# Sparse attention of a whole-model kernel: the order of its first heads, and the turn of the weights by diagonals of gate over sum

## The reference, cut to what matters

```python
s_c = q . kc * scale + bias_c;  p_c = softmax(where(valid_c, s_c, NEG_INF)) * any_c;  o_c = p_c @ vc
s   = q . ks * scale + bias;    o_s = softmax(s) @ vs        # selected blocks: all of the past
s   = q . kw * scale + bias_w;  o_w = softmax(s) @ vw        # window of 512: all of the past
gt  = sigmoid(gates)
o   = gt[..., 0:1] * o_c + gt[..., 1:2] * o_s + gt[..., 2:3] * o_w
```

## Time and profile before

| what | us |
|---|---|
| median of 3 runs | 3545.63 (3542.86 to 3548.09) |
| profiled execution | 3545.68 |
| its span, first to last instruction | 3543.9 |
| TensorE busy | 3438.5 (97%) |
| VectorE busy | 2297.3 (65%) |
| ScalarE busy | 1788.3 (50%) |

### The profile page before, as it was taken

The page is one execution under the profiler, slowest core; times in us unless marked ns, Lnnn a source line. Parts: engine busy times, 40 slices in busy tenths (PEclk is TensorE's granted clock), DMA queues, the critical chain, the costliest instruction groups (busy, mean ns, idle before and its releaser), DMA issues.

```text
span 3543.9 us, 62898 instructions
## 1 busy us (share of the span) xinstructions
PE 3438.5 (97%) x21968; PEld 2998.0 (85%) x21968; DVE 2297.3 (65%) x3449; ACT 1788.3 (50%) x2742; POOL 489.5 (14%) x538
## 2 busy tenths in 40 slices
PE   9998999999999999999999999999489999999999
PEld 7886888888888888887888888888378888888888
DVE  5788565555555766775666677778855765565565
ACT  4477464545454554553555444444444554444454
POOL 0001410111114100123100001105012000001105
PEclk9999999999999999999999999999899999999999
DMA  6562545565556555553456556667235455555555
GB/s 212 172 184 61 190 151 192 186 191 185 190 183 194 170 188 170 162 168 119 145 193 197 187 189 196 202 222 246 59 125 186 147 190 191 185 187 193 181 187 195
DMA packets 190644, 626.52 MB, mean 177 GB/s; under 512 B 26822, under 2 KB 40328, under 8 KB 190360
## 3 DMA queue, kind: packets, MB, share of 16 engines
q1 hardware_dynamic: 179948, 612.29, 53.9%
q10 hardware_dynamic: 10572, 12.56, 1.2%
HBM read 620.32 MB, written 3.15 MB: 176 GB/s over the span
## 4 chain that ended last, share of the span: by engine, by line
PE 88%; DVE 7%; ACT 2%; DMA 1%; issue 1%; POOL 0%; SPq 0%; ACTq 0%; DVEq 0%; POOLq 0%
PE bank L1943 54%; PE bank L1946 28%; PE m L1966 1%; DVE w_lo L1073 1%; DMA w_raw<-stream 1%; PE m L1956 1%; PE m L1968 1%; DVE prod L1749 1%; ACT w_hi L481 0%; DVE st L1752 0%; DVE st L1754 0%; DVE y L1100 0%; DVE w_lo L1077 0%; ACT s_first L666 0%; ACT u_own L972 0%
## 5 line engine op out<-in xcount | busy, mean ns | idle before, releaser
L1073 DVE TENSOR_TENSOR w_lo<-w_raw,w_hi 128x1024 fp32r<-128x1024 f32 x1086 | 1336.4, 1253 | 776.5 <-ACT w_hi L481 770.2
L1943 PE MATMUL bank<-act,w_hi 128*128 128x512 f32 x6016 | 1512.8, 393 | 3.6 <-DVE w_lo L1073 1.6
L481 ACT ACTIVATE w_hi<-w_raw 128x1024 fp32r<-128x1024 f32 x1090 | 1129.5, 1054 | 409.8 <-PE bank L1946 362.6
L1943 PEld LDWEIGHTS bank<-act,w_hi 128*128 128x128 f32 x6016 | 1082.7, 189 | 204.6 <-DVE w_lo L1073 4.3
L1946 PEld LDWEIGHTS bank<-act,w_lo 128*128 128x128 f32 x6016 | 820.8, 190 | 58.9
L1946 PE MATMUL bank<-act,w_lo 128*128 128x256 f32 x6016 | 838.7, 282 | 0.0
L1943 PE MATMUL bank<-ffn,w_hi 128*128 128x512 f32 x2432 | 613.5, 393 | 4.0 <-DVE w_lo L1077 2.7
L490 ACT ACTIVATE low<-bank 128x256 f32<-128x256 f32 x542 | 207.5, 383 | 745.0 <-PE bank L1946 744.1
L1943 PEld LDWEIGHTS bank<-ffn,w_hi 128*128 128x128 f32 x2432 | 436.2, 189 | 83.2 <-DVE w_lo L1077 5.0
L1946 PEld LDWEIGHTS bank<-ffn,w_lo 128*128 128x128 f32 x2432 | 333.9, 190 | 25.1
L1081 DVE TENSOR_TENSOR ev<-bank,low 128x256 f32<-128x256 f32 x468 | 198.2, 423 | 236.7 <-ACT low L490 233.3
(11 more groups left out here) (425 smaller groups left out, 2236.8 us busy)
## 6 DMA issues: line engine op xcount, KB each, us to landing
w_raw<-stream SPq DMA_DIRECT2D x1148, 512.0 KB, 3.5
b_part<-s_bt ACTq DMA_DIRECT2D x16, 256.0 KB
bias<-toeplitz SPq DMA_DIRECT2D x4, 512.0 KB, 9.1
pow_b<-powers ACTq DMA_DIRECT2D x8, 256.0 KB
pow_b<-powers ACTq DMA_DIRECT2D x16, 128.0 KB
res<-x_t SPq DMA_DIRECT2D x2, 512.0 KB, 9.0
res<-x_t ACTq DMA_DIRECT2D x2, 512.0 KB, 11.0
bias<-toeplitz SPq DMA_DIRECT2D x4, 256.0 KB, 11.7
```

The costliest lines, as they stand in the source:

```text
L481: a(w_hi[:, q, :], w_raw[:, q, :], ACT.Copy).then_inc(hi_ready, 1)
L1073: e.tensor_tensor(w_lo[:, q, :], w_raw[:, q, :], w_hi[:, q, :].bitcast(F32), ALU.subtract).then_inc(lo_ready, 1)
L1943: mm(bank[w][:, 0:2 * n], w_hi[:, q, wt], x(h * hk + k, 0, 2 * n), start=(h == 0 and k == 0), stop=False)
```

## The change

- Bias: SP loads the bias in two steps. The part of the first four heads (`FIRST_HEADS`) goes out between the first and the second load of the last `cmp` pair, the rest behind that pair. VectorE waits for each part only where it is used.
- Order ahead of the loop: pair 0's scores come ahead of the compression's matmuls on TensorE, and pair 1's behind them. The compression's results go into bank `m[4]`, the gates into `m[5]`. The sum of the LRU's squares is made during and right behind the compression, and the root is taken ahead of the gelu. VectorE splits a weight quarter ahead of the LRU's product.
- Order in the loop: VectorE is one head further: iteration `it` makes the scores and maxima of head `it + 1`, and head 0's come ahead of the loop. TensorE issues a pair's scores ahead of a turn instead of behind it. Copying the compressed keys and values comes behind head 0's exponentials, the compressed scores around head 0's turn, and their softmax in iterations 2 and 3. Compressed weights are turned ahead of heads 2, 3, 5, 7, 9, 11, 13 and 15 (`TURN_AFTER`).
- The turn: the weights keep their exponentials. VectorE makes four 128x128 diagonals a head (`scaler`, identity times factor, one 128x512 instruction, two heads' worth of memory), and TensorE multiplies each block of the exponentials with its diagonal, as an ordinary fp32 matmul.
- The fillers behind the compressed scores (22) and ahead of head 1's turn (10) are gone.

```diff
--- before
+++ after
...
+    scaler = at("scaler", A + 70, [P, 2, 4, P])
...
     score_bank = [m[0:2], bank]
+    FIRST_HEADS = 4
+    TURN_AFTER = (2,) + tuple(range(3, NH, 2))
...
-            sp_eng.wait_ge(halves_used, 4 * PH["in1"][1])
-            sp_eng.wait_ge(sem("toep_out"), 16)
-            for lo_c, hi_c, off in ((128, 384, 127), (0, 128, 255)):
-                for p0 in range(0, P, ROWS):
-                    src = bass.AP(toeplitz.tensor, off - p0, [[383, ROWS], [384 * ROWS, NH], [1, hi_c - lo_c]])
-                    sp_eng.dma_start(bias[p0:p0 + ROWS, :, lo_c:hi_c], src).then_inc(sem("bias_loaded"), 16)
+
+            def load_bias(h0, h1, into):
+                for lo_c, hi_c, off in ((128, 384, 127), (0, 128, 255)):
+                    for p0 in range(0, P, ROWS):
+                        src = bass.AP(toeplitz.tensor, off - p0 + 384 * ROWS * h0,
+                                      [[383, ROWS], [384 * ROWS, h1 - h0], [1, hi_c - lo_c]])
+                        sp_eng.dma_start(bias[p0:p0 + ROWS, h0:h1, lo_c:hi_c], src).then_inc(into, 16)
+
+            for q in range(4):
+                sp_eng.wait_ge(lo_ready, 4 * (after_in1 - 1) + (q - 3))
+                load(after_in1 - 1, q)
+                if q == 0:
+                    sp_eng.wait_ge(halves_used, 4 * PH["in1"][1])
+                    sp_eng.wait_ge(sem("toep_out"), 16)
+                    load_bias(0, FIRST_HEADS, sem("bias_steps"))
+            load_bias(FIRST_HEADS, NH, sem("bias_loaded"))
...
+            hi(c0 + 1, 0)
             block_high(1)
...
-            hi(c0 + 1, 0)
+            hi(c0 + 1, 1)
+            hi(c0 + 1, 2)
             lru_square(0, 3)
-            hi(c0 + 1, 1)
-            lru_square(3, 6)
-            hi(c0 + 1, 2)
-            lru_square(6, 8)
             hi(c0 + 1, 3)
+            lru_square(3, 8)
+            root_table()
+            norm("lru", z, 8, lru_n, LT * P, None)
             hidden(0)
             hidden(1)
             a(counted[:, 0:1], eps_col[:, :], ACT.Copy).then_inc(low_copied, 4)
+            a(exp_use[:, :], eps_col[:, :], ACT.Exp)
...
-            root_table()
-            s.wait_ge(sem("blk_ready"), 1)
-            s.wait_ge(sem("cmp_mm"), 3)
...
-            a(v_cmp[:, :], m[4][0:NCMP, 64:320], ACT.Copy).then_inc(sem("cmp_cp"), 1)
-            norm("lru", z, 8, lru_n, LT * P, None)
-            a(exp_use[:, :], eps_col[:, :], ACT.Exp)
+
+            def compressed_copies():
...
+                s.wait_ge(sem("cmp_mm"), 3)
...
+                a(v_cmp[:, :], m[4][0:NCMP, 64:320], ACT.Copy).then_inc(sem("cmp_cp"), 1)
...
+                if hh in TURN_AFTER:
+                    j = TURN_AFTER.index(hh)
+                    s.wait_ge(sem("pct_mm"), j + 1)
...
                 if it == 0:
+                    compressed_copies()
+                if it == 3:
                     s.wait_ge(sem("cmp_vec"), 3)
                     a(p_cmp[:, :, :], p_cmp[:, :, :], ACT.Exp).then_inc(sem("cmp_exp"), 1)
...
+            lo(c0, 3)
...
             e.tensor_tensor(z[:, 0:LT, :], lru_i[:, :, :], z[:, LT:2 * LT, :], ALU.mult).then_inc(sem("lru_vec"), 1)
-            c0 = PH["cmp"][0]
-            lo(c0, 3)
+            lo(c0 + 1, 0)
             block_low(1)
-            lo(c0 + 1, 0)
...
+            def score(hh):
+                if hh == 0:
+                    v.wait_ge(sem("bias_steps"), 16 + 32 * P // ROWS)
+                if hh == FIRST_HEADS:
+                    v.wait_ge(sem("bias_loaded"), 32 * P // ROWS)
+                if hh >= 4:
+                    v.wait_ge(sem("pt_mm"), 2 * hh - 6)
+                for at_ in range(2):
+                    v.wait_ge(sem("s_mm"), 4 * (hh // 2) + 2 * at_ + hh % 2 + 1)
+                    e.scalar_tensor_tensor(s_att(hh)[:, at_, :], score_bank[hh % 2][at_][:, 0:384], HD ** -0.5, bias[:, hh, :],
+                                           ALU.mult, ALU.add).then_inc(sem("s_bias"), 1)
+
...
+            v.wait_ge(sem("tok_cp"), 3)
+            score(0)
+            top(0)
+            top_negated(0)
             for it in range(NH + 1):
 
-                b, o = it % 2, (it + 1) % 2
-                if it < NH:
-                    if it >= 4:
-                        v.wait_ge(sem("pt_mm"), 2 * it - 6)
-                    for at_ in range(2):
-                        v.wait_ge(sem("s_mm"), 4 * (it // 2) + 2 * at_ + b + 1)
-                        e.scalar_tensor_tensor(s_att(it)[:, at_, :], score_bank[b][at_][:, 0:384], HD ** -0.5, bias[:, it, :], ALU.mult, ALU.add).then_inc(sem("s_bias"), 1)
+                o = (it + 1) % 2
+                if it + 1 < NH:
+                    score(it + 1)
                 if it:
                     v.wait_ge(sem("att_exp"), it)
                     e.reciprocal(stat[:, 112 + 8 * o:116 + 8 * o], stat[:, 96 + 8 * o:100 + 8 * o]).then_inc(sem("att_inv"), 1)
-                if it < NH:
-                    v.wait_ge(sem("s_bias"), 2 * it + 2)
...
+                if it + 1 < NH:
+                    top(it + 1)
...
-                if it < NH:
-                    v.wait_ge(sem("att_top"), 2 * it + 2)
...
-                if it == 0:
-                    compressed()
+                if it + 1 < NH:
+                    top_negated(it + 1)
+                if it == 3:
+                    compressed_weights()
                 if it == 3:
                     lo(c0 + 2, 0)
                 if it:
                     v.wait_ge(sem("att_fac"), it)
-                    for qb, c in enumerate((slice(0, 128), slice(128, 384))):
-                        f = stat[:, 128 + 8 * o + 2 * qb:130 + 8 * o + 2 * qb]
-                        e.tensor_tensor(s_att(it - 1)[:, :, c], s_att(it - 1)[:, :, c],
-                                        f.unsqueeze(2).to_broadcast([P, 2, c.stop - c.start]), ALU.mult).then_inc(sem("att_p"), 1)
-
+                    if it >= 3:
+                        v.wait_ge(sem("pt_mm"), 2 * it - 4)
+                    e.tensor_tensor(scaler[:, o, :, :], ident[:, :].unsqueeze(1).to_broadcast([P, 4, P]),
+                                    stat[:, 128 + 8 * o:132 + 8 * o].unsqueeze(2).to_broadcast([P, 4, P]), ALU.mult).then_inc(sem("att_p"), 1)
+                if it == 2:
+                    compressed_scores()
                 if it == 3:
                     v.wait_ge(root_taken, n_lru)
...
+            pe.wait_ge(sem("lru_sig"), 2 * LT)
+            pair_scores(0)
...
+            for kv in range(2):
+                pe.wait_ge(sem("blk_ready"), kv + 2)
+                i = PH["cmp"][0] + kv
+                into = m[4][0:60, T * kv:T * kv + T]
+                for q in range(4):
+                    if kv and q == 3:
+                        pe.wait_ge(sem("tok_cp"), 3)
+                        lru_sum(0, 3)
+                    pe.wait_ge(lo_ready, 4 * i + q + 1)
...
+                    for n in range(4):
...
+                        mm(into, high, w_hi[:, q, wt], start=(k == 0), stop=False)
...
+            lru_sum(3, 8)
+            pair_scores(1)
...
-            lru_sum(0, 2)
             turn_hidden(1)
-            pair_scores(0)
             pe.wait_ge(sem("cmp_cp"), 2)
-            pe.wait_ge(sem("tok_cp"), 3)
...
-            lru_sum(2, 8)
-            pe.wait_ge(sem("cmp_cp"), 5)
-            for b in range(2):
...
-            last.then_inc(sem("cmp_scores"), 1)
-            keep_busy(22)
+                if b:
+                    last.then_inc(sem("cmp_scores"), 1)
...
-                if hh == 1:
-                    keep_busy(10, m[4])
                 if hh == NH - 1:
                     keep_busy(8, m[0])
-                pe.wait_ge(sem("att_p"), 2 * hh + 2)
...
                     for n in range(3):
-                        last = nc.tensor.transpose(m[2 + at_][:, 128 * n:128 * n + 128], s_att(hh)[:, at_, 128 * n:128 * n + 128], ident[:, :])
+                        last = mm(m[2 + at_][:, 128 * n:128 * n + 128], s_att(hh)[:, at_, 128 * n:128 * n + 128],
+                                  scaler[:, hh % 2, 2 * (n > 0) + at_, :], start=True, stop=True)
                     last.then_inc(sem("pt_mm"), 1)
...
             for it in range(NH + 2):
+                if it == 1:
+                    compressed_scores(0)
+                if it and it % 2 == 0 and it + 2 < NH:
+                    pair_scores(it // 2 + 1)
                 if 1 <= it <= NH:
-                    if it % 2:
-                        cmp_weights(it // 2)
+                    if it - 1 in TURN_AFTER:
+                        cmp_weights(TURN_AFTER.index(it - 1))
                     transposes(it - 1)
-                if it % 2 == 0 and it + 2 < NH:
-                    pair_scores(it // 2 + 1)
+                if it == 1:
+                    compressed_scores(1)
...
```

More of the change, by code:

```diff
@@ L421, in _ @@
         if "mix1" in plan:
-            with sp_eng.Fori(2, after_in1) as i:
+            with sp_eng.Fori(2, after_in1 - 1) as i:
                 for q in range(4):
@@ L1295, in _ @@
             block_low(0)
```

(54 more changed lines are left out.)

40 lines of the change are left out of this document (24 added, 16 removed).

## The result

| | us |
|---|---|
| before, median of 8 runs | 3545.04 (3540.97 to 3548.09) |
| after, median of 8 runs | 3553.87 (3551.79 to 3558.98) |
| ratio | 1.0026, 95% interval 1.0017 to 1.0035 |
| profiled execution of after, its span | 3553.73, 3551.9 |

The change costs 8.8 us (8.05 between the two profiled executions). The forecast was +4.0, the rival *the clock stays down* +9.9. The time is in the range, but nearer to that rival. At 0.26% above before it falls among the outcomes slower by over 0.2%, which the prediction had given 0.23.

The account below looks back on a forecast made before the run. The bias transfer bounds the start, and VectorE and ScalarE, waiting for each other, the loop. The terms 0.7 + 1.15 + 2.0 + 0.2 = 4.0 on 3545.68 gave 3549.7 us, range 3540 to 3558.

Parts of the forecast that it names:

- the clock stays down: Rival: 1.2 GHz from the compressed scores to pair 1's result costs 6 and 3.4 us; 3555.6 us; chance 0.20.
- Part 1: Up to head 0's exponentials: early bias hidden; exponentials start at 271.3, 3.9 us earlier than 275.20.
- Part 2: Relay from head 0's exponentials to head 2's turn: most of the lead goes; turn at 291.9, 0.7 us later.
- one fall in the relay: Between head 0's exponentials and head 2's turn: 4.6 us of work at half clock, 2.3 us lost.
- The bound of 6: Upper bound on the relay's clock loss: nearly all of its 7.8 us of work at half clock.
- The bound of 13.4: From head 2's turn to the end of pair 1's result: 13.4 us with a clock dip; 12.3 taken.
- Part 3: The loop, pair 1's result to pair 5's: pairs of 7.7 and 7.5 us, 30.4 in all, 2.0 later.
- The ring: Loop cycle of scores, VectorE's factor and diagonals, turn, result and next scores: 7.5 us a pair, 7.7 with ScalarE's weight splits.
- Part 4: The end: the last two turns grow, mostly hidden by the wait for the last exponentials; +0.2 us (0 to 1.3).
- The clock holds: Rival: matmul turns keep the clock up, head 2 turns at 288.3; 3545.0 us; chance 0.20.
- VectorE sets the pace: Rival: VectorE paces the loop, the lead stays and four pairs take 26.6 us; 3538.2 us; chance 0.10.
- The early bias brings nothing: Rival: a transfer still ends VectorE's wait at 272.8, 3.9 us more; 3553.6 us; chance 0.05.

Follow-up runs that it names:

- the experiment with the diagonals first: After plus fillers, shortened relay and bias behind the loads, with VectorE making diagonals ahead of the next head's maxima from iteration 4; 3538.95 us, ratio 0.9982.
- the kernel with the same code up to there: After with the compressed weights' exponentials moved earlier on ScalarE and VectorE's weight split put behind head 2's diagonals; ratio to before 1.0004.
- the delayed kernel: Before with 58 fillers added in TensorE's stream behind the last pair's result; 3557.48 us, ratio to before 1.0036.
- the kernel with fillers: After with fillers put back where TensorE idles (3, 6, 8 and 22); 3548.56 us, ratio to before 1.0011.

## Why the prediction came out as it did

**Part 1 was right in number, in part by luck.** The root is taken at 267.60 (267.5), head 0's exponentials begin at 271.85 (271.3). But the compression's matmuls ended at 265.4, not 263.9, held up by a late weight quarter, and only 10 passes of the LRU sum were left behind them (2.32 us), not 16 (3.6): two errors that nearly cancel. "I count it as hidden" was wrong of the early bias. It lengthened the weight loads beside it; with the bias moved behind them, head 0's exponentials begin 1.4 us earlier and the stage ends 6.3 us earlier in the profiled execution, the rest by way of the clock. The prediction had named a wait for a weight load between 250 and 262 as a sign against it, and only SP's issues as its cause.

**Part 2, the relay's work, was right, its clock was not.** From the end of head 1's turn to head 2's diagonals I had 281.7 to 289.6, 7.9 us; measured are 290.3 to 298.0, 7.7. The step that failed is "one fall in the relay at 4.6 us of work at half clock, 2.3 lost". The relay up to head 1's turn was to take 7.8 us and took 15.0 (275.32 to 290.31), and it began 1.4 later, partly because the networks' second layer ran slow as well. That is 8.6 less 0.2, in place of 2.3; head 2 is turned 6.2 later than forecast. I had sized the fall by the lengths of the old falls, of a kernel with 32 fillers; those were gone. The bound of 6 for "nearly all" was exceeded too: all of this work ran at half clock (7.2), and so did the second layer ahead of it.

**To pair 1's result** it took 15.4 us, where I had 12.3, with half clock from 293.2 until 306.9. The bound of 13.4 supposed one short fall.

**Part 3 was nearly right.** A turn is 12 passes in 1.50, with 0.112 a pass; the diagonals take 0.69. A pair takes 7.85 (7.5 to 7.7), and from pair 1's result to pair 5's 31.4 (30.4, bound 31.5). The ring was the right cause, as the experiment with the diagonals first shows; that ScalarE's exponentials belong in it no run shows apart. (Its 9.15 adds up to 9.27, which gives 7.76 a pair in place of 7.7.) **Part 4** was 0.44 (0.2).

**The sum.** The stage lost 14.5, the forecast 4.0. That the time rose by 8.8 and not by 14 is owed to the 6.5 us behind the stage, which no step of the prediction had. The total lies closer to the forecast than the mechanism deserves, and that is luck. By the prediction's own signs it was wrong: head 2 turned after 295 (298.08), half clock for more than 8 us (30.7), and waits for a weight load between 250 and 262 (up to 1.34). The wait of 4 us or more ahead of head 2's turn was there (6.12), a pair was slower than 7.4 to 7.7. Of the rivals, *the clock stays down* describes what happened: it had head 2's turn at 295.6, and its condition (the clock down at the first compressed score) was met. *The clock holds* fell: it was down for 30.7 us with matmul turns. *VectorE sets the pace* fell with the ring. *The early bias brings nothing* had the wrong mechanism, but the early bias did cost.

**Open.** Why the first fall of the clock lasts 17.1 us in after and 6.8 in the kernel with the same code up to there is not settled, nor why after's later stages give back 6.5 us. Falls of the clock that before has near 1620, 2477 and 2777 are missing in after. Their place depends on more than the delay, and their absence alone doesn't explain the 6.5: the delayed kernel lacks two of the three as well and gave back 0.6. All kernels here give back something (0.6 to 6.5), so before's own rest of the program, 3201.5, is the slowest of all.

## What to carry to other kernels

Fillers in a hand-written order can carry the clock through a relay between engines, where they fill the waits. When an order changes, count afresh where TensorE runs dry, and bound the fall by all the work that lies behind it, not by the old fall's length: here even 14 us of work without a gap ran at half clock. A transfer moved ahead "into a gap" must be weighed against the loads in flight beside it, by their landing and not their issue alone. And a stage's result is read at its own end: behind it, a few microseconds come and go with where the clock falls.

## What was not expected

- The clock fell at 272.8 behind 8 us in which TensorE was busy for 5.64, and stayed at half until 289.8, though TensorE had no gap from 275.32 to 290.31. In the kernel with fillers the same stretch ran at 1.00.
- Edits of different kinds (fillers, 2.6 us less waiting, 1.4 us of an earlier start) each gave 6.3 to 7.2 us in the stage, and each had 10 to 20 us less of half clock. Timed they gave 5.3, 7.0 and 3.0.
- The weight loads took 4.4 us from issue to landing, and 6.8 to 7.7 with 0.8 MB of bias among them; the last load landed later though it was issued at the same time.
